# Two buffers per pair of heads for the query decays, and own buffers for two tiles of the first MLP units

## What is computed

```python
def trunk(x, c, ...):
    for i in range(DEPTH):                       # 2 layers
        mod = (silu(c) @ ada_w[i] + ada_b[i]).reshape(..., 6, D_MODEL)
        hn = modulate(x, norm_g[i, 0], mod[:, 0], mod[:, 1])
        out, ... = mlstm_mixer(hn, ...) if i % 2 == 0 else conv_mixer(hn, ...)
        x = x + mod[:, 2][:, None, :] * out
        hn = modulate(x, norm_g[i, 1], mod[:, 3], mod[:, 4])
        f = jnp.square(jax.nn.relu(hn @ mlp_w_up[i])) @ mlp_w_down[i]
        x = x + mod[:, 5][:, None, :] * f

# one head of the mLSTM, for a chunk of tokens:
    s = (q @ k.T) * exp(dmat - m)
    num = s @ v + exp(inter - m) * (q @ C0)      # C0: state before the chunk
    C1 = decay * C0 + (a * k).T @ v
```

## Time and profile before

| | |
|---|---|
| Runs | 1366.29, 1365.83 and 1365.40 us; median 1365.83 |
| Profiled execution: own time | 1367.82 us |
| Its span, from first to last instruction | 1366.0 us |
| PE busy | 1314.0 us (96% of the span) |
| DVE, ACT, POOL busy | 729.8, 361.9 and 529.0 us (53%, 26%, 39%) |
| Mean granted clock of TensorE | 0.989 of full speed |
| Unit V with the heads | about 114 to 215 us of the span |
| First MLP unit of layer 0 | about 327 to 386 us |
| First MLP unit of layer 1 | about 951 to 1010 us |

### The profile page before, as it was taken

How to read it: one execution, slowest core, us unless ns; L and a number is a source line. 1 busy time by engine, 2 the same in 40 slices (tenths; PEclk the granted TensorE clock), 3 DMA queues, 4 the chain that set the end, 5 groups by cost and what they waited for, 6 DMA issues and landing times.

```text
span 1366.0 us, 26372 instructions
## 1 busy us (share of the span) xinstructions
PE 1314.0 (96%) x11593; PEld 1286.8 (94%) x11593; DVE 729.8 (53%) x1124; ACT 361.9 (26%) x560; POOL 529.0 (39%) x248
## 2 busy tenths in 40 slices
PE   5899999999899999999999999999899999999997
PEld 4799889999899999999999999999899999999996
DVE  2724445677941531531549719859871551641774
ACT  3532442122311221221222432122321221211311
POOL 2433433443334343343344344434344444443440
PEclk9999999999999999999999999999999999999998
DMA  9665214753455546446443233332223332322321
GB/s 331 214 190 142 67 53 117 235 165 115 135 176 170 162 149 184 149 152 194 141 125 96 59 93 96 91 95 78 62 78 96 91 93 79 92 88 84 93 63 66
DMA packets 239804, 169.34 MB, mean 124 GB/s; under 512 B 5691, under 2 KB 211775, under 8 KB 239562
## 3 DMA queue, kind: packets, MB, share of 16 engines
q1 hardware_dynamic: 215946, 121.33, 30.3%
q10 hardware_dynamic: 23584, 46.27, 10.2%
q0 software_dynamic: 160, 0.07, 0.0%
HBM read 160.70 MB, written 6.94 MB: 123 GB/s over the span
## 4 chain that ended last, share of the span: by engine, by line
PE 81%; DVE 11%; issue 3%; ACT 2%; DMA 1%; POOL 1%; ACTq 0%; SPq 0%; POOLq 0%; DVEq 0%
PE G L1542 54%; PE G L1568 19%; PE B L1638 3%; DVE hb L1135 1%; DVE acc L1012 1%; DVE small_s L1482 1%; DVE yc L1481 1%; DMA xin<-in_x_sample 1%; PE B L1528 1%; DVE Xl L1149 1%; PE B L1833 1%; PE B L1907 1%; DMA batch<-in_ada_w 1%; DVE sqb L974 1%; PE B L1836 1%
## 5 line engine op out<-in xcount | busy, mean ns | idle before, releaser
L833 POOL TENSOR_TENSOR wl<-raw,wh 128x1024 fp32r<-128x1024 f32 x192 | 488.3, 2547 | 673.1 <-ACT wh L462 670.1
L462 ACT ACTIVATE wh<-raw 128x1024 fp32r<-128x1024 f32 x192 | 203.0, 1057 | 472.4 <-PE G L1542 228.9
L1542 PE MATMUL G<-Xh,wh 128*128 128x272 f32 x960 | 205.3, 295 | 5.0 <-ACT stage L469 4.0
L1542 PE MATMUL G<-Xl,wh 128*128 128x272 f32 x960 | 199.3, 289 | 0.0
L1542 PE MATMUL G<-Xh,wl 128*128 128x272 f32 x960 | 198.2, 288 | 0.0
L1542 PE MATMUL G<-Hh,wh 128*128 128x272 f32 x864 | 179.2, 289 | 0.0
L1542 PE MATMUL G<-Hl,wh 128*128 128x272 f32 x864 | 178.7, 288 | 0.0
L1542 PE MATMUL G<-Hh,wl 128*128 128x272 f32 x864 | 176.9, 286 | 0.0
L1542 PEld LDWEIGHTS G<-Xh,wh 128*128 128x128 f32 x960 | 150.3, 189 | 10.9 <-issue 8.7
L991 DVE TENSOR_TENSOR small_s<-G,modT 128x32 f32<-128x32 f32 x80 | 15.3, 191 | 265.5 <-PE G L1542 190.2
L1542 PEld LDWEIGHTS G<-Xl,wh 128*128 128x128 f32 x960 | 151.9, 190 | 0.0
(11 more groups left out here) (326 smaller groups left out, 2012.0 us busy)
## 6 DMA issues: line engine op xcount, KB each, us to landing
raw<-in_mlp_w_up SPq DMA_DIRECT2D x64, 512.0 KB, 4.0
raw<-in_mlp_w_down SPq DMA_DIRECT2D x64, 512.0 KB, 3.6
batch<-in_ada_w ACTq DMA_DIRECT2D x56, 512.0 KB, 5.1
raw<-in_mlstm_w_in SPq DMA_DIRECT2D x24, 512.0 KB, 4.4
raw<-in_conv_w_in SPq DMA_DIRECT2D x24, 512.0 KB, 3.8
aring<-in_ada_w ACTq DMA_DIRECT2D x22, 512.0 KB, 5.0
early<-in_ada_w SPq DMA_DIRECT2D x16, 512.0 KB, 12.0
raw<-in_mlstm_w_out SPq DMA_DIRECT2D x8, 512.0 KB, 4.8
```

Source lines behind the costliest of these rows:

```text
L462: nc.scalar.activation(wh[:, t % SLOTS], raw[:, t % RAWS], ACT.Copy).then_inc(s_hi, 1)
L833: nc.gpsimd.tensor_tensor(wl[:, t % SLOTS], raw[:, t % RAWS], wh[:, t % SLOTS].bitcast(F32), ALU.subtract).then_inc(s_lo, 1)
L1542: last = mm(G[:, 2 * (g % 2) + hf, 0:HALF], w[:, s, k, :], x[:, k, hf * HALF:(hf + 1) * HALF], start=st, stop=en)
```

## The change

**Heads.** `qt` becomes four buffers: `qdec[0..1]` for the spread decays and `qsc[0..1]` for the scaled queries, each chosen by a % 2. The copy to `decs` is gone, and `states` reads its three scalars from the columns of `qdec`. `scaled_queries(a)` for a of 1 to 3 moves on DVE from head 2a, ahead of `states`, to the end of head 2a-1, behind `head_done`. `query_decays(a)` for these moves on ACT from value tile 2a to value tile 2a-1, and waits for the states of head 2a-3 (for a = 1: for the read-out of the sample rows) and no longer for the last product of the pair ahead. `states` no longer waits for the scaled queries; `head_product` does. `qsc` lies in the region of `adaT`/`sel` and `qdec` in that of `selp`, both used up by then.

**First MLP units.** Tiles 3 and 4 are read out to buffers of their own, `own[0]` and `own[1]`, in both layers, and so wait for PE alone. Tile 5 goes to `stage[1]` as soon as tile 1 is drained, tile 6 to `stage[0]` as soon as tile 0 is, tile 7 to `stage[1]` as soon as tile 5 is. DVE reads the tiles where they now lie.

```diff
-        qt = sb("qt", [P, SEQ - P], at=at_n)
+        qdec = [sb(f"qdec{i}", [P, SEQ - P], at=at_n + i * 4096) for i in range(2)]
+        qsc = [sb(f"qsc{i}", [P, SEQ - P], at=at_row + (KT * GW + i * (SEQ - P)) * 4) for i in range(2)]
-        decs = sb("decs", [P, NJ - 1], at=at_n + 3104)
+        own = [sb(f"own{i}", [P, TOK], at=at_f + ... + i * ROW) for i in range(2)]
+        OWN = {FIRST - 1: acc, FIRST: own[0], FIRST + 1: own[1]}
...
+            def to_own(func):
+
+                def evac(t, g, j, per_t, per_g):
+                    m = g % KT
+                    act.wait_ge(s_used, t + 1)
+                    if m in OWN:
+                        dst = OWN[m]
+                    else:
+                        act.wait_ge(s_dr, g - m + {5: 2, 6: 1, 7: 6}[m])
+                        dst = stage[g % 2]
+                    nc.scalar.activation(halves(dst[:, :]), slot(g), func).then_inc(s_ev, 1)
+                return evac
...
             def query_decays(a):
 
-                if a:
-                    act.wait_ge(s_pv, 2 * a)
+                if a >= 2:
+                    act.wait_ge(s_st, 2 * a - 2)
+                elif a:
+                    act.wait_ge(s_srw, 1)
...
-                    nc.scalar.dma_start(qt[...], edec[...]).then_inc(s_qin, 16)
+                    nc.scalar.dma_start(qdec[a % 2][...], edec[...]).then_inc(s_qin[a % 2], 16)
...
-                    if m % 2 == 0:
-                        query_decays(m // 2)
+                    if m % 2 and m < H - 1:
+                        query_decays((m + 1) // 2)
...
-            first_unit(1, T_MLP0, G_MLP0, 0, 1, first_relu, to_stage(ACT.Relu), ada=5)
+            first_unit(1, T_MLP0, G_MLP0, 0, 1, first_relu, to_own(ACT.Relu), ada=5)
...
-                    first_unit(3, T_MLP1, G_MLP1, 1, 1, first_relu, to_stage(ACT.Relu))
+                    first_unit(3, T_MLP1, G_MLP1, 1, 1, first_relu, to_own(ACT.Relu))
...
             def scaled_queries(a):
-                dve.wait_ge(s_qin, 32 * (a + 1))
-                chain.link(V.tensor_copy(decs[:, :], qt[:, P - 1:SEQ - P:P]))
-                V.tensor_tensor(qt[:, :], qT[:, a, P:SEQ], qt[:, :], ALU.mult).then_inc(s_qe, 1)
+                dve.wait_ge(s_qin[a % 2], 32 * (a // 2 + 1))
+                if a >= 2:
+                    dve.wait_ge(s_pv, 2 * a - 2)
+                V.tensor_tensor(qsc[a % 2][:, :], qT[:, a, P:SEQ], qdec[a % 2][:, :], ALU.mult).then_inc(s_qe, 1)
...
             def states(h):
...
-                dve.wait_ge(s_qe, h // 2 + 1)
+                decs = lambda i: qdec[h // 2 % 2][pr, i * P + P - 1:i * P + P]
...
-                if h % 2 == 0:
-                    scaled_queries(h // 2)
+                if h == 0:
+                    scaled_queries(0)
                 states(h)
                 if h:
                     head_done(h - 1)
+                if h % 2 and h + 1 < H:
+                    scaled_queries((h + 1) // 2)
...
                 pe.wait_ge(s_st, h + 1)
+                pe.wait_ge(s_qe, a + 1)
```

More of the change, by code:

```diff
@@ L240, in build_program @@
         XP2 = [sb(f"XP2{i}", [P, KT, 2 * XH], F32R, at=at_f + i * KT * 2 * XH * 4) for i in range(2)]
+        own = [sb(f"own{i}", [P, TOK], at=at_f + 2 * KT * 2 * XH * 4 + D * 4 + KT * 2 * NSEQ * 4 + i * ROW) for i in range(2)]
+        OWN = {FIRST - 1: acc, FIRST: own[0], FIRST + 1: own[1]}
         XP = (None, XP1, XP2, XP2)
@@ L306, in build_program @@
         s_kt, s_ktd = sem("keys_turned"), sem("keys_turned_out")
-        s_em, s_qin = sem("query_decays_out"), sem("query_decays_in")
+        s_em, s_qin = sem("query_decays_out"), [sem(f"query_decays_in{i}") for i in range(2)]
         s_qe, s_u, s_st = sem("queries_scaled"), sem("chunk_products"), sem("chunk_states")
@@ L538, in scaled_in @@
             def scaled_in(o, g):
-                return acc[:, :] if o == 2 else stage[g % 2][:, :]
+                return OWN.get(o, stage[g % 2])[:, :]
             def first_relu(n, o, g):
@@ L671, in query_decays @@
                     h = 2 * a + h2
[L672 removed]
+                    nc.scalar.dma_start(qdec[a % 2][DK * h2:DK * (h2 + 1), :], edec[h:h + 1, :].broadcast_to((DK, SEQ - P))).then_inc(s_qin[a % 2], 16)
             def maxima_out():
@@ L967, in drain @@
                         dve.wait_ge(s_ev, at(g + 1, j, per))
-                        ps = o = halves(acc[:, :] if scaled and m == 2 else stage[g % 2][:, :])
+                        ps = o = halves((OWN.get(m, stage[g % 2]) if scaled else stage[g % 2])[:, :])
                     else:
@@ L1117, in scale_first @@
                 ps = G[:, 2 * (g % 2):2 * (g % 2) + 2, :]
-                s = acc[:, :] if o == 2 else stage[g % 2][:, :]
+                s = OWN.get(o, stage[g % 2])[:, :]
                 V.tensor_copy(bcol[:, o:o + 1], ps[:, 0, XH - 1:XH])
@@ L1296, in states @@
                 for i in range(1, NJ - 1):
-                    chain.link(V.scalar_tensor_tensor(Sst[pr, i, :], Sst[pr, i - 1, :], decs[pr, i - 1:i],
+                    chain.link(V.scalar_tensor_tensor(Sst[pr, i, :], Sst[pr, i - 1, :], decs(i - 1),
                                                       B7[pr, i * DVA:(i + 1) * DVA], ALU.mult, ALU.add))
-                V.scalar_tensor_tensor(Cfin[pr, h // 2, :], Sst[pr, NJ - 2, :], decs[pr, NJ - 2:NJ - 1], B6[pr, 0:DVA],
+                V.scalar_tensor_tensor(Cfin[pr, h // 2, :], Sst[pr, NJ - 2, :], decs(NJ - 2), B6[pr, 0:DVA],
                                        ALU.mult, ALU.add).then_inc(s_st, 1)
@@ L1835, in head_product @@
                 for jt in range(1, NJ):
-                    last = mm(out[jt], qt[pr, (jt - 1) * P:jt * P], Sst[pr, jt - 1, :], start=False, stop=True,
+                    last = mm(out[jt], qsc[a % 2][pr, (jt - 1) * P:jt * P], Sst[pr, jt - 1, :], start=False, stop=True,
                               skip_group_check=True)
```

1 line of the change is left out of this document (added).

## The result

The changed kernel takes **1354.11 us** in the median (1353.74 to 1354.53, 4 runs), beside 1366.06 us (1365.4 to 1369.53, 4 runs) for the kernel before on the same chip: a ratio of 0.9906, 95% interval 0.9895 to 0.9918. That is 12.0 us faster, where 14.2 were forecast. The profiled execution took 1354.53 us, 13.3 less than that of before.

A forecast was written before the change was run, and what follows sets the result against it. PE was taken as the bound nearly everywhere, so only its gaps and low clock could be won: 4.3 + 6.5 - 0.5 + 6.6 - 2.7 = 14.2 us, taking the median from 1365.83 to 1351.6 us; range 1348.3 to 1356.5.

The forecast's parts named there:

- the rival of one fall of the clock: PE's clock falls in a new gap of 2.5 to 2.7 us; one fall gives 1353.9 us; chance 0.27.
- Heads, 4.3 us: Heads 2, 4 and 6: without DVE's copy and with its multiplication earlier, PE's waits for states go, winning 4.3 us.
- Tile 5, 6.5 and 6.6 us: First MLP units: tile 5 starts when tile 4 ends, winning 6.5 us in layer 0 and 6.6 in layer 1.
- The new gap in layer 1, 2.7 us: Down projection's second step: PE stands 2.7 us because tile 7's read-out waits for DVE's drain of tile 5.
- Five overlaps with POOL: Layer 1's six DVE drains: five instructions meet a POOL subtraction, 2.13 us each; bounds four and six.
- one of the prediction's own signs of being wrong: PE's clock: a stretch at 0.50 behind either of the new gaps would show the forecast wrong.
- The wait for `batch`, -0.5: Layer 0, ahead of the `batch` products: the 2.01 us wait stays and grows by 0.5 us, loads falling into a shorter stretch.

The follow-up runs named there:

- the trace with the late issue: Changed kernel with DVE's copy and multiplication ahead of the states again and ACT's decay-load issue behind the heads' last product; 1356.97 us, ratio 0.9927.
- the heads alone: Changed kernel with tiles 3 and 4 of the MLP units back in `stage`, only the heads' part kept; 1363.34 us, ratio 0.9965.
- the kernel with the issue at even tiles: Changed kernel with decay loads issued at even value tiles, without the product wait, and the multiplication ahead of the states, no copy; 1354.13 us, ratio 0.9908.

## Why the prediction was right, and where it was not

The time lies 2.5 us above the forecast, within the range, and nearest to the rival of one fall of the clock, which gave 1353.9. Point by point:

- **Heads, 4.3 us: right in size, wrong in cause.** They won 4.6. The step that failed is the one that charged the whole wait to DVE's copy and multiplication, and gave no price to the issue of 1.10 us that "delayed ACT's copy of the head's result". With DVE's two instructions put back and the issue early nothing is lost; with the issue behind the product as well 3.2 of the 4.6 us come back. The chain is issue, copy of the head's result, factors, POOL's mask, POOL's subtraction, and DVE held by it. That the size came out owes nothing to the cause named: it was taken from head 0, where nothing of this chain is late, and the same change happened to move the issue too. That part is luck. The comparison with head 0 didn't tell the two causes apart, as there neither the issue nor the subtraction stands in the way. A row that shows it was there to be read: ACT's copy of the result, 1.8 us behind the start of the issue at 136.46, is ended by no engine but by ACT's own issuing, and DVE stands 3.81 us for it.

```profile
138.25 0.66 ACT L714 ACTIVATE num<-B 128x258 f32<-128x258 f32 x2 [3.02 <-issue]
```

  Whether taking both of DVE's instructions away would have been enough, with the issue left late, no run shows. Without the copy alone the hold passes to the multiplication and 0.6 us are won. An estimate from the trace with the late issue says that it might have been: there DVE has finished the weights at 146.45 and PE ends its products of keys and values at 147.49 (the row below), so the states, whose first instruction reads PSUM and so wouldn't be held (last section), could start some 1.1 us ahead of 148.69, about the whole gap of 1.02.

```profile
146.40 1.09 PE L1842 MATMUL B<-vtok,ktok 128*64 128x129 f32 x8
```

- **Tile 5, 6.5 and 6.6 us: right.** 6.45 in layer 0, and 6.7 in layer 1 where nothing takes its place. Tile 5 starts 0.26 us behind the last pair of tile 4 (the second row is its first), at full clock:

```profile
358.33 0.42 PE L1589 MATMUL G<-Yh,wl 128*128 128x272 f32 x2
358.59 0.41 PE L1563 MATMUL G<-Yh,wh 128*128 128x272 f32 x2
...
358.00:360.00 2.00, 2.00 (x18) 2.00 (x18) 1.97 (x2) 1.23 (x2) 1.65 (x2) 1.00 0.87 279
```

- **The new gap in layer 1, 2.7 us: right in place, cause and size.** 2.45, and 2.38 to 2.50 in the seven other kernels' executions with this buffer rule. Five overlaps with POOL were forecast and are there; the six drains take 23.8 us where 24.0 were reckoned. Giving tile 7 another buffer removes it.
- **The clock behind that gap: the rival's chance was too low.** The forecast put no fall there, at 0.42 against 0.27. In eight executions with the gap the clock fell six times, that of the changed kernel among them, and so one of the prediction's own signs of being wrong is there, a stretch at 0.50 behind a new gap. A fall cost 1.5 us (106.2 against 104.7), not the 2.3 taken from the longer stretches of before.
- **The wait for `batch`, -0.5: wrong in sign, and within noise.** 0.96 us, where 2.5 was expected; the other executions with the new order show 0.5 to 1.2, and one 2.18. The kernel before shows 2.01 and 1.02, and the heads alone 1.63. The step that took one execution's 2.01 for the kernel's was too bold. That the loads come into a busier stretch, 289 GB/s from 360 to 374 us where before had 221, didn't make them late.
- **The start.** The first scores stand between 115.7 and 118.9 us in all executions, whatever the kernel. The profiled execution of after lost 1.66 us there to that of before. This, with the fall and less the better wait, is most of the difference between 14.2 and 13.3.

By the terms: 14.2 + 0.3 (heads) + 1.5 (`batch`) - 1.2 (layer 1) - 1.7 (start) + 0.1 for the rest gives 13.2, against 13.3 between the profiled executions. The medians differ by 12.0 in the first comparison and by 12.9 in the second; the forecast of 14.2 lies above both by about one fall of the clock.

## What to carry to other kernels

When two engines are late together, look for what both wait on: an instruction that stands between a product and its copy delays every engine behind that copy. Here moving it away won 3.2 us with the two instructions next to the gap in place, and taking the longer of these away won 0.6. Undo the parts one at a time before you name the cause of a gain, since the comparison with an undisturbed iteration removes several causes at once.

When a buffer is added to take away one wait, write down for every tile which drain frees its buffer, to the last tile of the unit: here the wait moved from tile 5 to tile 7, and one more line of the same table gave the other 4 us (1350.7 us). Judge a transfer's wait of 1 or 2 us from several executions.

## What the runs showed of the hardware

- **A gap of 2 to 2.5 us of PE is followed by a fall of the clock in some executions and not in others.** 2.38 and 2.50 us kept 1.00; 2.40, 2.41, 2.44, 2.45, 2.48 and 2.38 (the kernel with the issue at even tiles) fell. The wait for `batch` of 2.01 us kept it, one of 2.18 us didn't:

```profile
380.48 5.37 PE L1655 MATMUL B<-batch,cpad 128*32 128x128 f32 x128 [2.18 <-DMA batch<-in_ada_w]
...
382.00:384.00 2.00, 2.00 (x45) 2.00 (x40) 0.47 (x1) 2.00 (x3) 0.93 (x1) 0.50 0.07 21
```

  There the same 128 products took 5.37 us instead of 3.70. All six gaps of 4.0 us (two each in the kernel before, in its second execution and with the heads alone) had a fall, of 3.4 or of 6.8 us. Length alone doesn't decide it in this range, and a forecast does well to price such a gap with the fall.
- **The fall can come after the gap.** In the changed kernel it began 1 us after PE had begun again, and lasted 3.4 us in which PE was busy throughout.
- **Instructions of DVE that read SBUF alone were held to the end of POOL's subtraction, and those with an operand in PSUM were not.** In the trace of the changed kernel some 80 instructions with inputs in SBUF alone start inside such a subtraction, 0.3 us or more ahead of its end, and every one of them ends behind it; some 20 with an operand in PSUM start there too, and none is longer than elsewhere. The copy of three columns took 0.14, 1.14 or 1.82 us in the heads, and the multiplication 0.56, 1.53 or 2.21, as more or less of the subtraction was left. The Trainium skill ("SBUF — State Buffer", SBUF: two separate sides) calls the port pair that GpSimd and VectorE share an exclusive lock, which whoever starts first holds for its whole instruction, against VectorE's instructions with two SBUF inputs and those in a two-port mode; and "VectorE: DVE Perf Modes" (Mode 2×_2P) puts a copy with one SBUF input among the latter, in fp32 too. The trace agrees: the copy ended 0.02 and 0.03 us behind the subtraction, the multiplication 0.42 us. The weights of a head, with one operand in PSUM (`B`) and one in SBUF, lie wholly inside the subtraction in head 2 of the changed kernel and take their usual 0.67 us:

```profile
142.88 2.39 POOL L851 TENSOR_TENSOR wl<-raw,wh 128x1024 fp32r<-128x1024 f32 x1 [0.15 <-ACT wh L465]
...
143.57 0.67 DVE L1306 SCALAR_TENSOR_TENSOR dexp<-B,dexp 128x512 f32<-128x512 f32 x1
```
